# The sixteen exchange DMAs of an activation block issued as eight and eight, with one W chunk between

## What is computed

```
def sqrelu_mlp(h, w1, w2):
    return jnp.square(jax.nn.relu(h @ w1)) @ w2
...
    h2 = rmsnorm(x, g_mlp[l])
    u = jax.nn.relu(jnp.einsum('bsd,df->bsf', h2, w_up[l]))
    x = x + jnp.einsum('bsf,fd->bsd', u * u, w_down[l])
```

## Time and profile before

| | |
|---|---|
| median of 3 runs | 2108.51 us (2106.99 to 2113.06) |
| the profiled execution: its own time, its span | 2109.23 us, 2107.4 us |
| TensorE matmul busy | 2035.2 us, 97% |
| VectorE busy | 1281.6 us, 61% |
| ScalarE busy | 1037.9 us, 49% |
| DMA queue of SP | 475.86 MB, its packets take 65.8% of 16 engines' span |
| mean granted TensorE clock | 0.986 |

### The profile page before, as it was taken

The page is one execution under the profiler, slowest core; times in us unless marked ns, Lnnn a source line. Parts: engine busy times, 40 slices in busy tenths (PEclk is TensorE's granted clock), DMA queues, the critical chain, the costliest instruction groups (busy, mean ns, idle before and its releaser), DMA issues.

```text
span 2107.4 us, 23130 instructions
## 1 busy us (share of the span) xinstructions
PE 2035.2 (97%) x8901; PEld 1647.6 (78%) x8901; DVE 1281.6 (61%) x1309; ACT 1037.9 (49%) x1369; POOL 19.2 (1%) x24
## 2 busy tenths in 40 slices
PE   3999889999999999999999999999999999999998
PEld 1777568788888888887788777888888888888887
DVE  7989776656665554556546656655555554554555
ACT  3333434544444444545666755555445544544554
POOL 0000010000000000000000000000000000000000
PEclk9899889999999999999999999999999999999999
DMA  9999896877776566664556455556666665756663
GB/s 400 413 387 376 328 345 218 312 242 248 285 240 191 196 220 186 218 215 160 175 171 213 138 174 189 180 180 213 207 199 196 213 210 175 240 204 199 205 215 120
DMA packets 228886, 484.42 MB, mean 230 GB/s; under 512 B 17672, under 2 KB 38600, under 8 KB 219952
## 3 DMA queue, kind: packets, MB, share of 16 engines
q1 hardware_dynamic: 226768, 475.86, 65.8%
q0 software_dynamic: 848, 3.70, 0.6%
q10 hardware_dynamic: 1168, 3.46, 0.4%
HBM read 459.87 MB, written 2.10 MB: 219 GB/s over the span
## 4 chain that ended last, share of the span: by engine, by line
PE 80%; DVE 7%; DMA 7%; ACT 2%; SPq 2%; issue 1%; ACTq 0%; DVEq 0%
PE ps L523 25%; PE ps L525 25%; PE ps L524 25%; DMA raw<-in_w_mod 3%; DVE scr L1387 3%; SPq L377 2%; DVE w_low L1375 2%; DMA raw<-in_fnet_w 2%; PE ps L578 1%; ACT w_high L957 1%; PE ps L615 1%; DVE scr L1402 1%; PE ps L591 0%; DMA extra<-scr 0%; DMA raw<-in_w_mlp_in 0%
## 5 line engine op out<-in xcount | busy, mean ns | idle before, releaser
L1375 DVE TENSOR_TENSOR w_low<-raw,w_high 128x1024 fp32r<-128x1024 f32 x672 | 816.5, 1222 | 680.2 <-ACT w_high L957 679.9
L957 ACT ACTIVATE w_high<-raw 128x1024 fp32r<-128x1024 f32 x672 | 706.0, 1058 | 864.1 <-PE ps L525 732.1
L523 PE MATMUL ps<-w_high,h_both 128*128 128x512 f32 x1536 | 607.6, 396 | 11.9 <-DVE w_low L1375 6.9
L525 PE MATMUL ps<-w_high,h_both 128*128 128x512 f32 x1536 | 600.7, 391 | 0.0
L524 PE MATMUL ps<-w_low,h_both 128*128 128x512 f32 x1536 | 600.6, 391 | 0.0
L523 PE MATMUL ps<-w_high,u_high 128*128 128x512 f32 x1152 | 450.2, 391 | 4.7 <-DVE w_low L1375 4.0
L525 PE MATMUL ps<-w_high,u_low 128*128 128x512 f32 x1152 | 449.0, 390 | 0.0
L524 PE MATMUL ps<-w_low,u_high 128*128 128x512 f32 x1152 | 449.0, 390 | 0.0
L523 PEld LDWEIGHTS ps<-w_high,h_both 128*128 128x128 f32 x1536 | 290.3, 189 | 76.7 <-issue 8.7
L525 PEld LDWEIGHTS ps<-w_high,h_both 128*128 128x128 f32 x1536 | 290.0, 189 | 61.3
L524 PEld LDWEIGHTS ps<-w_low,h_both 128*128 128x128 f32 x1536 | 290.5, 189 | 60.5 <-issue 1.4
(11 more groups left out here) (188 smaller groups left out, 819.8 us busy)
## 6 DMA issues: line engine op xcount, KB each, us to landing
raw<-in_w_mod SPq DMA_DIRECT2D x96, 1024.0 KB, 7.5
raw<-in_w_mlp_in SPq DMA_DIRECT2D x64, 1024.0 KB, 5.8
raw<-in_w_mlp_out SPq DMA_DIRECT2D x64, 1024.0 KB, 5.6
raw<-in_w_up SPq DMA_DIRECT2D x64, 1024.0 KB, 5.5
raw<-in_w_down SPq DMA_DIRECT2D x64, 1024.0 KB, 5.2
raw<-in_w_in SPq DMA_DIRECT2D x48, 1024.0 KB, 5.3
raw<-in_fnet_w SPq DMA_DIRECT2D x16, 1024.0 KB, 7.1
extra<-scr SPq DMA_DIRECT2D x512, 32.0 KB, 1.9
```

The source lines that it names most:

```text
L523: eng.matmul(dst, ah, wh, start=(k == 0), stop=False)
L525: last = eng.matmul(dst, al, wh, start=False, stop=(k == KT - 1))
L957: eng.activation(w_high[:, h % LEAD, :], raw[:, slot, (h % 2) * 2 * CW:(h % 2 + 1) * 2 * CW], ACT.Copy).then_inc(high_ready, 1)
L1375: eng.tensor_tensor(w_low[:, h % LEAD, :], raw[:, slot, piece], w_high[:, h % LEAD, :].bitcast(f32), ALU.subtract).then_inc(raw_used if h ...
```

## The change

The sixteen DMAs of an exchange are issued in two parts. The first part (block rows 0 and 1) keeps its place and its wait for `t_blocks`. The second part (block rows 2 and 3) is issued behind the next W chunk, and so behind that chunk's wait for a free slot. Where a `w_mod` tile stands between that chunk and the second part's place, the second part comes behind the tile too. In the first quarter the order, which was chunk 12, sixteen, chunk 13, tile, chunk 14, sixteen, chunk 15, chunk 16, tile, sixteen, chunks 17 to 19, becomes chunk 12, eight, chunk 13, tile, eight, chunk 14, eight, chunk 15, eight, chunk 16, tile, eight, chunk 17, eight, chunks 18 and 19. In the second quarter the first exchange stood behind chunk 9, ahead of chunk 10 and a tile; its second part is now behind that tile, and the other three second parts are behind chunks 14, 18 and 22.

```diff
-            def exchange(c):
-
-                t.add("blocks")
-                eng.wait_ge(t_blocks, t.at("blocks", 0))
-                for a in range(QUADS):
+            def exchange(c, part):
+
+                if part == 0:
+                    t.add("blocks")
+                    eng.wait_ge(t_blocks, t.at("blocks", 0))
+                for a in range(2 * part, 2 * part + 2):
                     for q in range(QUADS):
                         eng.dma_start(exchanged[q * BLOCK:(q + 1) * BLOCK, a * RUN:(a + 1) * RUN],
...
                 for c, y in enumerate(UP_ENDS):
-                    if ch == y // 2 + EXCHANGED_BEHIND:
-                        exchange(c)
+                    for part in range(2):
+                        if ch == y // 2 + EXCHANGED_BEHIND + part:
+                            exchange(c, part)
...
                 for c, y in enumerate(FIRST_UP_ENDS):
-                    if pos + 2 == y // 2 + EXCHANGED_BEHIND - 1:
-                        exchange(c)
+                    for part in range(2):
+                        if pos + 2 == y // 2 + EXCHANGED_BEHIND - 1 + part:
+                            exchange(c, part)
```

## The result

| | before | after |
|---|---|---|
| median (11 runs each) | 2108.72 us (2106.86 to 2113.06) | 2113.76 us (2109.72 to 2119.51) |
| ratio after to before, 95% interval | | 1.0026 (1.0017 to 1.0034) |
| the profiled execution: time, span | 2109.23, 2107.4 us | 2111.27, 2109.5 us |
| TensorE matmul busy | 2035.2 us | 2033.6 us |

A forecast was written before the change was run, and what follows sets the result against it. TensorE, busy 2035.2 of 2107.4 us, was taken as the bound, with 5.6 us to win at two stops. Terms -3.5 + 2.8 + 1.6 = +0.9 gave 2110.1 for the profiled execution, 2109.4 as median; range 2104.5 to 2114.0.

The forecast's parts named there:

- the second half late behind its load: Rival, chance 0.15: every second group of the first two quarters lands behind a loaded queue and half 30 stops; 2115.0 us.
- First quarter, exchange 0: First MLP's first exchange: second group lands at 339.1 behind two loads, moving ScalarE's take from 336.66 to 339.1.
- Exchange 1 ... last landing 347.9 + 4.43 + 1.9: First quarter's next exchange: last landing 354.3 for 351.8, half 30 at 358.9 exactly when due, no stop.
- Exchange 2 and chunk 17: First quarter: chunk 17 goes out at 362.6 for 365.07, half 34 0.6 late, half 36 about 0.6 more.
- First quarter -3.5: First-quarter sum: 4.7 us lost before, 1.2 after, so 3.5 us gained; bounds -4.7 and 0.
- Second quarter, exchange 0 ... last landing 498.6 + 1.9: Second quarter's first exchange: last landing 500.5, ScalarE's take about 500.6 for 498.56, 2.0 late.
- The stops: Second quarter: 0.9 us new at half 26 plus half 34's, 3.65 in all for 0.90 before; +2.8 us.
- The clock term: Second quarter: a 2.8 us gap at half 34 brings a clock fall like the first quarter's, +1.6 us.
- The other 24 exchanges: nothing: First MLP's quarters three and four and the second MLP: later landings stay hidden, as takes may begin 6.3 us later.
- The undisturbed quarters pay: Rival, chance 0.03: the other 24 exchanges each cost what a take comes beyond 6.3 us; 2116 us.
- nothing moves: Rival, chance 0.05: raw slots hold SP and both TensorE stops remain as they are; 2108.5 us.
- The chunk is all that matters: Rival, chance 0.17: the second quarter's loss does not appear; -3.5 to -5.6 us, 2103.0 to 2105.0.

The follow-up runs named there:

- exchange 2 alone: The changed kernel with only exchange 2 of the first quarter split, around chunk 17, and all others whole: 2103.69 us, ratio 0.9982 to before.
- first quarter only: The changed kernel with the split kept only in the first quarter of the first MLP, whole exchanges elsewhere: 2109.31 us, ratio 1.0001 to before.
- second quarter only: The changed kernel with the split kept only in the second quarter of the first MLP, whole exchanges elsewhere: 2114.01 us, ratio 1.0025 to before.
- GpSimd late: Against the changed kernel, GpSimd issues the second eight in the first two quarters after SP's eight land; other exchanges whole: 2141.32 us, ratio 1.0156 to before.
- the small loads: The changed kernel with loads between two parts in the first two quarters reading a quarter of their bytes: 2107.74 us, ratio 1.0003 to before.
- other quarters only: The changed kernel with the split kept only in the first MLP's quarters three and four and the second MLP's four: 2108.82 us, ratio 1.0010.
- four, then twelve: The changed kernel with four DMAs in the first part of each exchange and twelve in the second: 2112.15 us, ratio 1.0019 to before.
- twelve, then four: The changed kernel with twelve DMAs in the first part of each exchange and four in the second: 2127.64 us, ratio 1.0092 to before.
- second part on GpSimd at once: Against the changed kernel, GpSimd issues the second eight beside SP's eight in the first two quarters; other exchanges whole: 2101.96 us, ratio 0.9972 to before.

## Why the prediction was wrong

Forecast was 2109.4, range 2104.5 to 2114.0, with "the same" likeliest at 0.85. The time of 2113.76 lies at the upper edge of the range. A difference of 5.0 us is still "the same" in the prediction's own terms (under 6.3), but it is a clear slowing, and not 0.9. What happened is close to the second rival, *the second half late behind its load*, which I gave 0.15 and priced at 0 + 6.5, 2115.0. Measured is -0.4 + 6.0, with chunk 17 no earlier and half 30 stopping, as that rival says.

- **"First quarter, exchange 0", the landing, is the step that failed.** The issue was right: last issue forecast at 336.0, measured at 332.4 + 3.57 = 336.0. I took the load's own landing of 8.0 us as what holds the exchange ("331.1 + 8.0 = 339.1, which I take; bounds 337.9 and 340.5"). Measured is 5.2 us from the last issue, 10.0 from the tile's: take 0 at 341.2, outside my bounds. The tile was itself the second load in flight behind a chunk, and it landed 8.7 us after its issue, so the exchange is whole about 1.3 us behind it. That a load behind a load takes longer was in the earlier trace rows (5.9 the first, 8.0 the second of two); that the small DMAs come behind the second one, and not with it, was left out of the sum.
- **"Exchange 1 ... last landing 347.9 + 4.43 + 1.9"** took the 1.9 us of a free queue for a part behind a chunk. Measured are 2.8 to 3.0. Of its lateness of 3.0 us at the take, 2.1 are inherited and 0.9 are its own. Half 30 "due at 358.9: no stop, and no slack left" was exact on the slack, and so every microsecond beyond the forecast became a stop: it started at 358.03 + 3.57 = 361.6, 2.7 late, of which 2.13 stand as a gap there and the rest in earlier gaps and restarts.
- **"Exchange 2 and chunk 17"**: out at 365.5 and not 362.6, because the group started 3.0 us late (360.5, forecast 357.5). The split saved its 5.06 us, and the two landings ahead took them back. With the two left whole (exchange 2 alone) the group keeps its start and the saving is 4.8 us. *First quarter -3.5* came out as -0.4. Counted from start to start of the matmuls, against the usual 0.23 us, the three stops cost 0.5 + 2.4 + 1.1 us (a gap in brackets leaves out 0.2 to 0.3 us of each stop) and a late start at 375.92, half 36, that shows no gap 0.4 more: 4.4 in all. The one stop of before costs 4.9 in the same count, 1.6 of it clock. That the clock stayed full behind the 2.13 us was luck as far as the runs tell: in the kernel with the first quarter only it fell behind 2.08, and no gain was left.
- **"Second quarter, exchange 0 ... last landing 498.6 + 1.9"**: the issue was right again (494.6 + 4.01, the shift there, is 498.6), the landing was 4.4. It is the same order, chunk and tile ahead, for which I had used 8.0 from the tile in the first quarter; I priced the two alike orders by two rules. Take 0 came at 503.0 (forecast 500.6), half 18 stopped for 1.10, and half 26 started at 531.5 where 528.0 was forecast.
- **The stops**, forecast 3.65 in all, came as 1.10 + 2.99 + 0.78 = 4.9, and the large one stood at half 26, not 34. **The clock term**, +1.6, came as 1.3 us, from start to start, but behind another stop than forecast; the 6.0 are 4.0 of stops, 1.3 of clock and the rest in restarts. The clock term does not simply add to the stops: in the kernel with the second quarter only, the gap at half 26 was 3.34 us and 13 matmuls ran at half clock, twice as many, and then half 34 did not stop at all; its second leg, 165.46, is the same. What the clock took at half 26 was there time that half 34 would have waited anyway. The table by stretch shows the level, 0.50 of the full clock (1.2 GHz), for the six matmuls behind the gap of the change:

```profile
527.50:530.20 2.70, 2.69 (x6) 2.15 (x7) 2.60 (x2) 2.67 (x4) 0.00 (x0) 0.50 0.17 8
```

- **"The other 24 exchanges: nothing"** held, by the stretches of after and by the kernel that splits them alone. *The undisturbed quarters pay* and *nothing moves* did not happen. *The chunk is all that matters* is true of one exchange out of 32, split alone.

The rule of the Trainium skill that I had used (DMA: Bandwidth & Descriptors, Queues, rings and completion order: a DMA engine takes the descriptors of one ring in ring order) gave the right direction, with the split working against itself. It does not reach the kernel with GpSimd late, whose DMAs have a ring of their own and took 5.7 to 7.2 us. The same section also says that an engine takes turns between queues, packet by packet, and that the increment of a semaphore lands only after all earlier writes of its DMA engine, across its queues. The second fits these 5.7 to 7.2 us. No run here parts waiting for data from waiting for the increment.

**Left open.** How much of the delay is the small DMA's data waiting its turn, and how much its semaphore; and how the 7.4 us of the small loads divide.

## What to carry to other kernels

In this kernel small DMAs on a critical chain are best issued ahead of large loads, from either queue: the exchanges 0 and 1 that were looked at are whole 7.5 to 10.1 us after the load's issue, with eight or with four of their DMAs behind it. A split that lets an urgent load pass pays where that load is the late one and the next exchange does not follow at once (exchange 2: -4.5 us); done everywhere it cost 5.0. Where issue time is the cost, a second idle queue that issues at once, ahead of the load, gives both (-6.2 us, the lowest here). And a chain whose forecast ends with "no slack left" is priced by the error of its landings: here 2.1 and 0.9 us in series made chunk 17 3.0 us late.

## What was not expected of the hardware

- Whether and when the clock falls does not follow from the length of the gap ahead of it. Behind gaps of 2.60 us (371.43 in the second quarter only) and 2.99 us (527.51 in the change) the first matmul already ran at half clock. Behind 3.10 us (372.88 before), 2.70 (371.98 in the other quarters only), 2.13 (527.68 in four, then twelve) and 2.08 us (361.22 in the first quarter only) two to five matmuls ran first and then it fell. Behind 2.13 us (358.03 in the change) and 2.69 us (347.88 in twelve, then four) it stayed full. Behind 4.39 us, in the latter kernel, the third matmul was the first to be slow:

```profile
366.18 0.50 PE L526 MATMUL ps<-w_high,h_both 128*128 128x512 f32 x1 [4.39 <-DVE w_low L1378]
366.52 0.39 PE L527 MATMUL ps<-w_low,h_both 128*128 128x512 f32 x1
366.75 0.53 PE L528 MATMUL ps<-w_high,h_both 128*128 128x512 f32 x1
367.07 0.63 PE L526 MATMUL ps<-w_high,h_both 128*128 128x512 f32 x1
```

- GpSimd issued these 32 KB DMAs faster than SP: 3.93 us for eight against 5.05 (exchange 0, second part on GpSimd at once and late), 0.49 against 0.63 each.
- A 32 KB transfer from SBUF to SBUF, 1.8 us from issue to landing at the end of a whole exchange, takes up to 7.5 us where two 1 MB loads were issued 2.6 and 3.2 us before it (twelve, then four).
